# Long convolution and forgetting attention on one Trainium2 core: projections in another order, every tap on VectorE, probabilities scaled by ScalarE

## The reference

```python
h = rms_norm(x, mix_norm)
a, g, q, k, v, fl = split(h @ w_in)            # 512 columns each, fl has 8
u = a * sigmoid(g)                             # conv_module
y = causal depthwise conv of u, 31 taps, + conv_b
y_conv = silu(layer_norm(y, ln_g, ln_b))
cum = cumsum(log_sigmoid(fl + forget_b))       # forgetting_attention
s = q @ k.T / 8 + cum[query] - cum[key], causal
y_attn = softmax(s) @ v
y = concat([rms_norm(y_conv), rms_norm(y_attn)])
x = x + y @ w_out
```

## Time and profile before

| | |
|---|---|
| median of 3 runs | 1732.27 us (1729.11 to 1732.4) |
| the profiled execution | 1733.64 us, of which the span is 1731.8 us |
| granted TensorE clock over the span | 0.961 |
| PE busy | 1604.0 us, 93% |
| DVE busy | 829.5 us, 48% |
| ACT busy | 792.9 us, 46% |
| POOL busy | 604.4 us, 35% |
| stage fox | from about 1375 to 1531 us of the span |

### The profile page before, as it was taken

One profiled execution on the slowest core, in us unless ns is written; L12 is line 12 of the kernel. 1 busy time (PEld: TensorE's weight loads), 2 busy tenths in 40 slices (PEclk: granted clock), 3 DMA queues, 4 the chain that ended last, 5 costly groups with the idle time before them and its releaser, 6 DMA issues.

```text
span 1731.8 us, 27558 instructions
## 1 busy us (share of the span) xinstructions
PE 1604.0 (93%) x10808; PEld 1466.4 (85%) x10808; DVE 829.5 (48%) x1036; ACT 792.9 (46%) x1087; POOL 604.4 (35%) x250
## 2 busy tenths in 40 slices
PE   8999888688899999999998999999999988699997
PEld 7999788587689998999986799998999875489997
DVE  4444455634364444444454554445444478654443
ACT  5444437322254444444465544445444564554443
POOL 2444203212024443544425144443444353224442
PEclk9999999888899999999999999999999998799999
DMA  7455343100125444455542344444554442225542
GB/s 268 184 183 185 141 179 125 73 1 1 37 100 212 186 181 147 183 188 188 190 157 76 110 182 182 182 182 149 212 188 180 159 146 98 82 101 213 187 177 90
DMA packets 48081, 259.93 MB, mean 150 GB/s; under 512 B 5376, under 2 KB 5632, under 8 KB 27296
## 3 DMA queue, kind: packets, MB, share of 16 engines
q1 hardware_dynamic: 47664, 258.77, 40.6%
q10 hardware_dynamic: 288, 0.34, 0.1%
q0 software_dynamic: 80, 0.14, 0.0%
HBM read 258.18 MB, written 1.05 MB: 150 GB/s over the span
## 4 chain that ended last, share of the span: by engine, by line
PE 81%; ACT 7%; DVE 7%; issue 2%; POOL 2%; DMA 1%; SPq 0%; DVEq 0%; ACTq 0%; POOLq 0%
PE banks L357 71%; ACT gu_hi L328 2%; DVE gu_lo L337 1%; PE banks L1229 1%; PE banks L1235 1%; DMA raw_gu<-units_gu 1%; POOL dn_lo L350 1%; DVE arena L2276 1%; ACT arena L394 1%; DVE x L485 1%; PE banks L1202 1%; ACT h_hi L377 1%; PE banks L1170 0%; PE banks L1926 0%; ACT dn_hi L333 0%
## 5 line engine op out<-in xcount | busy, mean ns | idle before, releaser
L350 POOL TENSOR_TENSOR dn_lo<-raw_dn,dn_hi 128x1024 fp32r<-128x1024 f32 x154 | 519.3, 3372 | 909.9 <-ACT dn_hi L333 891.0
L357 PE MATMUL banks<-h_hi,gu_hi 128*128 128x256 f32 x2256 | 642.5, 285 | 15.3 <-DVE h_lo L417 8.9
L357 PE MATMUL banks<-h_lo,gu_hi 128*128 128x256 f32 x2256 | 640.3, 284 | 0.0
L357 PE MATMUL banks<-h_hi,gu_lo 128*128 128x256 f32 x2256 | 640.3, 284 | 0.0
L337 DVE TENSOR_TENSOR gu_lo<-raw_gu,gu_hi 128x2048 fp32r<-128x2048 f32 x161 | 371.6, 2308 | 240.0 <-ACT gu_hi L328 239.6
L357 PEld LDWEIGHTS banks<-h_hi,gu_hi 128*128 128x128 f32 x2256 | 433.5, 192 | 23.3 <-issue 8.6
L357 PEld LDWEIGHTS banks<-h_lo,gu_hi 128*128 128x128 f32 x2256 | 433.7, 192 | 4.8 <-issue 0.2
L357 PEld LDWEIGHTS banks<-h_hi,gu_lo 128*128 128x128 f32 x2256 | 433.5, 192 | 0.0
L328 ACT CAST gu_hi<-raw_gu 128x2048 fp32r<-128x2048 f32 x161 | 306.3, 1905 | 51.1 <-PE banks L357 27.6
L500 ACT ACTIVATE silu<-silu 128x256 f32<-128x256 f32 x132 | 55.2, 418 | 513.2 <-DVE silu L508 513.2
L357 PE MATMUL banks<-dn_hi,act_hi 128*128 128x512 f32 x528 | 207.4, 393 | 1.7 <-POOL dn_lo L350 1.7
(11 more groups left out here) (341 smaller groups left out, 1556.4 us busy)
## 6 DMA issues: line engine op xcount, KB each, us to landing
raw_gu<-units_gu SPq DMA_DIRECT2D x161, 1024.0 KB, 5.5
raw_dn<-units_dn SPq DMA_DIRECT2D x162, 512.0 KB, 3.3
x<-x_in SPq DMA_DIRECT2D x2, 512.0 KB, 5.0
raw_gu<-units_gu SPq DMA_DIRECT2D x2, 512.0 KB, 7.3
out<-x SPq DMA_DIRECT2D x1, 1024.0 KB, 3.9
cst<-constants SPq DMA_DIRECT2D x1, 784.0 KB, 12.3
lora<-low_rank SPq DMA_DIRECT2D x1, 512.0 KB, 13.1
arena<-final_gain SPq DMA_DIRECT2D x1, 512.0 KB, 4.2
```

Source lines behind the costliest of these rows:

```text
L350: nc.gpsimd.tensor_tensor(dn_lo[:, p, 0:n], raw_dn[:, p, 0:n], dn_hi[:, p, 0:n].bitcast(F32), ALU.subtract).then_inc(dn_lo_ready, 1)
L357: ins = nc.tensor.matmul(out, a, b, start=first and i == 0, stop=last and i == 2)
```

## The change

The weight order puts k ahead of the convolution's half 1, so that PE now projects: ag half 0, k, logits, q, ag half 1, v. `turn_u(1)` comes after the first scores. Both groups of scores use banks 0 to 3, so `scores(1)` waits for the exponentials of group 0; the transposed probabilities go to banks 6, 7 (group 0) and 0 to 3 (group 1), outputs to banks 6 and 7, `accT` to banks 4 and 5. All 31 taps are on DVE (124 instructions); `make_products`, POOL's additions and the addition of `acc2` are gone. ACT scales the probabilities (16 activations), where DVE had 8 multiplications; DVE keeps the reciprocals. ACT loads the table for Sigmoid ahead of the scaling, and the set `natural_log_exp_and_others` ahead of the second exponentials. POOL makes the low halves of dn of units 3 to 9 with nothing between. DVE's `lo_gu` of unit 9 stands behind the normalisation (L2375), no longer ahead of the statistics. PE waits for the last tap where it waited for `acc`. Left out below are the bank numbers, the lists of step names and the removed helpers `make_products` and `add_products`.

```diff
-    add(ag[0][6:8] + ag[1][0:2], ag[1][2:4])
-    add(ag[1][4:8], f)
-    add(k[0:4], k[4:6])
-    add(k[6:8] + q[0:2], q[2:4])
-    add(q[4:8], v[0:2])
+    add(ag[0][6:8] + k[0:2], k[2:4])
+    add(k[4:8], f)
+    add(q[0:4], q[4:6])
+    add(q[6:8] + ag[1][0:2], ag[1][2:4])
+    add(ag[1][4:8], v[0:2])
...
-        DVE_TAPS = LONG_TAPS - POOL_TAPS
-        TAP_SPLIT = ((5, 9, 13, 17), (3, 6, 9, 12, 16))
+        TAP_SPLIT = ((3, 5, 8, 11, 14, 16, 21, 22, 25, 26, LONG_TAPS), (2, 3, 10, 12, LONG_TAPS))
...
-            add_products(0, 3)
-            lo_dn_pool(pool, *unit(s, 3))
-            add_products(3, 7)
-            lo_dn_pool(pool, *unit(s, 4))
-            add_products(7, POOL_TAPS)
-            lo_dn_pool(pool, *unit(s, 5))
-            add_products(POOL_TAPS, POOL_TAPS + 3)
-            lo_dn_pool(pool, *unit(s, 6))
-            add_products(POOL_TAPS + 3, 2 * POOL_TAPS)
-            for u in (7, 8, 9):
+            for u in range(3, 10):
                 lo_dn_pool(pool, *unit(s, u))
...
+            def normalized(g, i):
+                wait(act, FX, "dve", ("recip", g, i))
+                for hh in (2 * i, 2 * i + 1):
+                    for b, cols in enumerate(BLOCKS_Q):
+                        part = f_probs[g][:, hh, cols]
+                        ins = nc.scalar.activation(part, part, ACT.Copy, scale=softmax_cols(g, "max")[:, hh, b:b + 1])
+                done(ins, ("probs", g, i))
...
             sigmoids(0)
-            hi_gu(act, *unit(s, 3))
             wait(act, FX, "pool", "pads")
             u_turned(0)
-            wait(act, FX, "act", ("uT", 0))
-            make_products(0, 3)
+            hi_gu(act, *unit(s, 3))
             hi_dn(act, *unit(s, 3))
-            sigmoids(1)
+            tokens_scaled("k", k_tok, 6, rstd)
+            hi_gu(act, *unit(s, 4))
             fox_there(act, s, "f")
             done(cp(f_rows, banks[0:HEADS, 2, 0:T]), "f")
-            hi_gu(act, *unit(s, 4))
-            u_turned(1)
-            make_products(3, 5)
+            hi_dn(act, *unit(s, 4))
             wait(act, FX, "dve", "nabs")
             done(nc.scalar.activation(FST["soft"], FST["soft"], ACT.Exp), "exp_f")
             wait(act, FX, "act", "exp_f")
             done(nc.scalar.activation(FST["soft"], FST["soft"], ACT.Ln, bias=const("ones")[:, 0:1]), "ln_f")
-            hi_dn(act, *unit(s, 4))
-            make_products(5, 7)
             hi_gu(act, *unit(s, 5))
-            tokens_scaled("k", k_tok, 4, rstd)
-            hi_dn(act, *unit(s, 5))
+            turned("kT", k_ch, 0)
             wait(act, FX, "pe", "cum")
             for at, n in ((0, P), (P, 2 * P)):
                 ins = nc.scalar.activation(c_rows[:, at:at + n], banks[:, 2, 256:256 + n], ACT.Copy, scale=-1.0)
             done(ins, "c_hi")
-            make_products(7, POOL_TAPS)
-            wait(act, FX, "act", ("uT", 1))
+            hi_dn(act, *unit(s, 5))
+            tokens_scaled("q", q_tok, 4, FST["rstd8"])
             hi_gu(act, *unit(s, 6))
-            turned("kT", k_ch, 0)
-            tokens_scaled("q", q_tok, 6, FST["rstd8"])
+            turned("qT", q_ch, 2)
             hi_dn(act, *unit(s, 6))
-            make_products(POOL_TAPS, POOL_TAPS + 2)
-            turned("qT", q_ch, 2)
-            hi_gu(act, *unit(s, 7))
-            make_products(POOL_TAPS + 2, POOL_TAPS + 5)
             exponentials(0, 0)
             exponentials(0, 1)
-            make_products(POOL_TAPS + 5, POOL_TAPS + 7)
+            nc.scalar.preload_act_table(ACT.Sigmoid)
+            normalized(0, 0)
+            normalized(0, 1)
+            sigmoids(1)
+            hi_gu(act, *unit(s, 7))
+            u_turned(1)
+            hi_dn(act, *unit(s, 7))
+            nc.scalar.preload_act_table_set("natural_log_exp_and_others")
+            exponentials(1, 0)
+            exponentials(1, 1)
+            turned_probs(0, 0)
+            normalized(1, 0)
+            normalized(1, 1)
+            turned_probs(0, 1)
+            hi_gu(act, *unit(s, 8))
             tokens_scaled("v", v_fox, 4, rstd)
-            hi_dn(act, *unit(s, 7))
-            exponentials(1, 0)
-            turned_probs(0, 0)
-            turned_probs(0, 1)
-            outputs(0)
-            exponentials(1, 1)
-            make_products(POOL_TAPS + 7, 2 * POOL_TAPS)
-            hi_gu(act, *unit(s, 8))
             turned_probs(1, 0)
             turned_probs(1, 1)
+            outputs(0)
+            outputs(1)
             hi_dn(act, *unit(s, 8))
-            outputs(1)
             hi_gu(act, *unit(s, 9))
...
-            def normalized(g, i):
+            def reciprocals(g, i):
                 wait(dve, FX, "act", ("exp", g, i))
                 heads = slice(2 * i, 2 * i + 2)
                 done(nc.vector.reciprocal(softmax_cols(g, "max")[:, heads, :], softmax_cols(g, "sum")[:, heads, :]),
                      ("recip", g, i))
-                wait(dve, FX, "dve", ("recip", g, i))
-                for b, cols in enumerate(BLOCKS_Q):
-                    part = f_probs[g][:, heads, cols]
-                    ins = tt(part, part, softmax_cols(g, "max")[:, heads, b:b + 1].to_broadcast(
-                        [P, 2, cols.stop - cols.start]), ALU.mult)
-                done(ins, ("probs", g, i))
...
             A, B = TAP_SPLIT
             gated(0)
-            lo_gu(dve, *unit(s, 3))
             wait(dve, FX, "act", ("uT", 0))
             taps(0, 0, A[0])
-            gated(1)
+            lo_gu(dve, *unit(s, 3))
             taps(0, A[0], A[1])
+            taps(0, A[1], A[2])
             lo_gu(dve, *unit(s, 4))
+            taps(0, A[2], A[3])
             wait(dve, FX, "pe", "fT")
...
-            taps(0, A[1], A[2])
+            taps(0, A[3], A[4])
...
             lo_gu(dve, *unit(s, 5))
-            taps(0, A[2], A[3])
+            taps(0, A[4], A[5])
             wait(dve, FX, "act", "c_hi")
...
+            taps(0, A[5], A[6])
             lo_gu(dve, *unit(s, 6))
-            taps(0, A[3], DVE_TAPS)
+            shifts(0, 0)
+            taps(0, A[6], A[7])
+            shifts(0, 1)
+            taps(0, A[7], A[8])
+            reciprocals(0, 0)
+            reciprocals(0, 1)
+            taps(0, A[8], A[9])
+            gated(1)
+            taps(0, A[9], A[10])
             wait(dve, FX, "act", ("uT", 1))
             taps(1, 0, B[0])
+            shifts(1, 0)
+            taps(1, B[0], B[1])
+            shifts(1, 1)
             lo_gu(dve, *unit(s, 7))
-            taps(1, B[0], B[1])
-            shifts(0, 0)
-            shifts(0, 1)
+            reciprocals(1, 0)
+            reciprocals(1, 1)
             taps(1, B[1], B[2])
-            normalized(0, 0)
-            normalized(0, 1)
+            outputs(0)
             taps(1, B[2], B[3])
-            shifts(1, 0)
-            shifts(1, 1)
-            outputs(0)
-            normalized(1, 0)
+            outputs(1)
+            lo_gu(dve, *unit(s, 8))
             taps(1, B[3], B[4])
-            lo_gu(dve, *unit(s, 8))
-            normalized(1, 1)
-            taps(1, B[4], DVE_TAPS)
-            for j in range(4):
-                wait(dve, FX, "dve", ("tap", DVE_TAPS - 1, j))
-            dve.wait_ge(products_added, 2 * (POOL_TAPS - 1))
-            done(tt(Fx["acc"], Fx["acc"], Fx["acc2"], ALU.add), "acc")
-            outputs(1)
-            lo_gu(dve, *unit(s, 9))
...
+            lo_gu(dve, *unit(s, 9))
...
-            project(4, (0, 1, 2, 3), gu(3), 0).then_inc(gu_used, 1)
+            w = gu(3)
+            project(4, (0, 1), w, 0)
             wait(pe, FX, "act", "f")
             for t in range(2):
                 ins = nc.tensor.transpose(banks[:, 3, 8 * t:8 * t + 8], f_rows[:, tokens(t)], ident[0:HEADS, 0:HEADS])
             done(ins, "fT")
-            turn_u(1)
+            project(4, (2, 3), w, 1024).then_inc(gu_used, 1)
+            wait(pe, FX, "act", ("uT", 0))
+            turn_heads("kT", k_tok, 0)
             project(4, (4, 5), dn(3), 0).then_inc(dn_used, 1)
-            w = gu(4)
-            done(project(4, (6, 7), w, 0), "k")
-            project(6, (0, 1), w, 1024).then_inc(gu_used, 1)
             wait(pe, FX, "dve", "logf")
             pe.wait_ge(fox_consts, 16)
             mm(banks[:, 2, 256:512], logf[:, 0, :], upto, start=True, stop=False)
             done(mm(banks[:, 2, 256 + P:512], logf[:, 1, :], upto[:, 0:P], start=False, stop=True), "cum")
+            w = gu(4)
+            done(project(4, (6, 7), w, 0), "q")
+            project(6, (0, 1), w, 1024).then_inc(gu_used, 1)
+            wait(pe, FX, "dve", "c_lo")
+            turn_heads("qT", q_tok, 2)
             project(6, (2, 3), dn(4), 0).then_inc(dn_used, 1)
-            project(6, (4, 5, 6, 7), gu(5), 0).then_inc(gu_used, 1)
-            wait(pe, FX, "act", ("uT", 1))
-            turn_heads("kT", k_tok, 0)
-            wait(pe, FX, "dve", "c_lo")
-            project(4, (0, 1), dn(5), 0).then_inc(dn_used, 1)
-            turn_heads("qT", q_tok, 2)
-            w = gu(6)
```

(48 more changed lines are left out.)

86 lines of the change are left out of this document (32 added, 54 removed).

## The result

| | before | after |
|---|---|---|
| median, first comparison (5 runs each) | 1729.11 us | 1718.34 us (1714.32 to 1719.44) |
| ratio, first comparison | | 0.9932, 95% interval 0.9909 to 0.9954 |
| median, second comparison (11 and 6 runs) | 1734.33 us | 1716.01 us |
| ratio, second comparison | | 0.9901, 95% interval 0.9878 to 0.9923 |
| the profiled execution | 1733.64 us | 1714.32 us, span 1712.3 us |

The account below looks back on a forecast made before the run. DVE's list of taps, stretched by GpSimd, was taken to bound stage fox. Last tap 10.2 us earlier plus 3.4 in the tail made 13.6 us off 1733.6: 1720.0, as a median 1719 (1715 to 1723; outer range 1710 to 1729).

Parts of the forecast that it names:

- DVE from the first tap to the last: DVE's list in stage fox: taps, low halves, maxima, small steps, GpSimd hold-up and waits sum to 93.4 us, last tap at 1488.4.
- The waits: DVE's in-order waits in stage fox: 3.1 at `gated(1)`, 4.0 at `outputs(0)`, 1.1 at `lo_gu(5)`, 0.4 small ones; sum 8.6 us.
- The lock: DVE held up by GpSimd's low halves of units 3 to 8: between 0 and 14.7 us, taken as 13.
- The wait of 16 us: PE ends output rows 4 and 5 near 1472, 16 us ahead of DVE's last tap, and stands waiting for it.
- my theory of the experiments: Stage fox: gain comes from silencing GpSimd's additions; new projection order costs and brings nothing; three tail loads worth 3.8 us.
- The tail: From the sum's transposes to the last sums of squares: 24.8 us before, 21.0 after; gain taken as 3.4 us.
- 3 loads on the path go, 3.8 us: ScalarE's roots in the tail: with the set loaded earlier, three table loads of 1.28 us leave the path, 3.8 us.
- The drain: The skill's 1380 ns beside each ScalarE table load, 2.66 us per switch; would give about 1717 us; not used in the sum.
- Longer waits: Rival: ScalarE's or PE's chain late at `gated(1)`, the shifts or `outputs(0)` by twice the waits; 1724 to 1728 us, chance 0.20.
- slower taps: Rival: DVE's taps stay at 0.64 us each whatever GpSimd does; last tap at 1505, 1737 us, chance 0.07.
- no change: Rival: PE's chain replaces the taps as bound, or table loads remain and waits double; 1729 to 1735 us, chance 0.08.
- shorter: Rival: low halves and taps overlap more, or the two long waits are absent; 5 to 9 us more, 1710 to 1715, chance 0.14.

## Why the prediction was right, and which of its terms were off

**DVE from the first tap to the last.** Forecast: first tap 3.2 us earlier, then 93.4 us. Measured: 3.1 us earlier, then 90.8 (1392.79 to 1483.56). By terms: the taps alone 0.398 to 0.404 each, as taken. The waits 3.4 at `gated(1)` (3.1), 4.0 at `outputs(0)` (4.0), 1.1 at `lo_gu(5)` (1.1): 8.8 with the small one at the first maxima, for 8.6. Scaling 0.36 for one (0.35). The lock: 10.7 for 13. That is the term that was mis-sized, and it makes 2.3 of the 2.6 us. Four of the six low halves cost the 2.0 to 2.15 us that I took from the rows; one fell beside maxima and one beside low halves of the outputs, which both read PSUM, and these cost 0.8 and 1.5.

**PE and the queues.** The wait of 16 us was 15.4; the order of the projections did cost nothing. But the new lists bring something, and there my theory of the experiments was too poor: in the kernel before with all taps on DVE the last tap stands 5.8 us later than in the changed kernel. Of this 3.1 are the first tap, which the changed kernel has earlier because ScalarE copies u ahead of `hi_gu(3)` and DVE takes taps ahead of `lo_gu(3)`. In the rest the traces differ in DVE's waits, 12.0 us there (3.3 for scores, 4.8 at `outputs(0)`) and 8.8 in the changed kernel. The sum held this without naming it, since it laid out the whole new list. Whether the order of projections is what shortens the waits, no run shows.

**The tail.** Forecast 3.4 us, measured 4.6. The mis-sized term is what the lower clock costs behind PE's wait. Transposes and row 6 together I put at 1.9 and 4.1; they took 1.6 and 3.5 (1483.61, 1485.23, 1488.76), so `yT` came 7.6 us after the transposes instead of 8.5. The further 0.4 that I kept for short waits was not needed. The size of this term is in part chance, as far as single executions tell: the kernel in which DVE scales had 4.75 for row 6. PE's wait ahead of row 0 was 1.4 for 1.5. The three loads that I priced at 3.8 were not worth that: without them off the path the changed kernel loses 1.3 to 1.4, because its first root is made while PE does row 6, so that only the last load is on the path; the likely cause is the new place of `outputs(1)`, by elimination. The step that failed was "3 loads on the path go, 3.8 us"; it did not spoil the sum, which built the new tail from its own pieces and never subtracted 3.8 from the old one.

**The drain** that the Trainium skill (ScalarE: Activation LUTs, What ACT_TABLE_LOAD costs) puts beside each load, 1380 ns, does not show: without the set Exp starts at 1488.45, 0.01 us after its load ends, and one load on the path lengthened the stage by 1.3 to 1.4 us in all.

**The rivals.** Longer waits, slower taps and no change did not come: the last 38 taps, with GpSimd silent, ran at 0.398 and not at 0.64. In the stage itself the truth lay towards "shorter": 17.3 us for 13.6, that is 2.5 in the taps and 1.2 in the tail. For the profiled execution I had 1720.0, and it took 1714.3: 3.7 of the 5.7 us are stage fox, the other 2.0 lie in stages that the change does not touch, 1.6 of them in the one told of below. The median of the first comparison, 1718.34, met the forecast within 0.4 us, and that is luck: the stage gained 3.7 us more than I summed, and the draw of the other stages took nearly all of that back. A stage shorter by 17.3 us asks for a ratio of 0.9900, which lies outside the first interval (0.9909 to 0.9954); the second comparison, at 1716.0 with the kernel before at 1734.3, has it (0.9901). So the mechanism and most terms held, and the total hit better than they did.

## What to carry to other kernels

Work given to GpSimd beside VectorE was no second engine here while both read SBUF: price it as VectorE's own time, all but a part (four additions beside taps took 4.04 us from it, a low half of dn 2.0 to 2.15, but 0.8 beside row maxima that read PSUM). Here some 23 us of additions were to spare 14.5 us of taps. When work is moved onto the bounding engine, its in-order waits for helpers become the next cost, so price each hand-over by the chain of the helper (scaling on ScalarE cost 1.4 us of the stage). Gains that shorten the same wait do not add: measure each alone in both kernels before summing.

## What the hardware showed that I had not expected

**The total goes with the clock in another stage.** In thirteen profiles, the stage that begins at about 202 us, which no kernel here touches, took either 281.6 to 284.7 us (seven times) or 286.0 to 288.4 (six times). It goes with the granted clock between 400 and 500 us, 0.92 to 0.93 in the short ones and 0.88 in the long ones, in both kernels and their variants alike. Both kernels' profiles, windows with the columns of the earlier trace rows, before and then after:

```profile
400.00:500.00 100.00, 88.33 (x596) 76.48 (x595) 39.28 (x68) 33.95 (x54) 9.44 (x4) 0.88 0.08 27
```

```profile
400.00:500.00 100.00, 88.28 (x626) 76.29 (x626) 39.99 (x70) 36.58 (x57) 9.46 (x4) 0.93 0.08 27
```

That is 1.6 of the 19.3 us between the two profiled executions, and it is as large as several terms here; what decides it is open.

**Who runs back to back keeps the other out.** In the kernel before with all taps on DVE, a low half on GpSimd that came 3 us into a run of 28 or 30 taps waited for all that were left of it (10.15 and 11.31 us for work of 2.4), not for the one that was running. The changed kernel shows it once: the low half at 1441.60, 2.5 us into ten taps, ends 2.2 us after the last of them and took 3.79. One that came ahead of a run, or within 0.2 us of its start (1416.80 for 1416.61), held DVE for some 2.1 us. No run varies the moment of arrival, so where the border lies is open.

**After one and the same wait PE's lower clock lasts differently long.** Behind 15.36 us of waiting, three products of row 6 came at a step of some 0.43 us in one execution, and nine in another (granted clock 0.50 in both). Only single executions show it here; what decides it is open.
